# Layer norm 1 folded into transposed tiles, and the per-layer gate in blocks of 512 columns, in a one-core encoder layer

## What is computed

```python
h = layer_norm(ALPHA * x + merged @ w_out, ln1_g, ln1_b)      # merged: attention | SSM, each RMS-normed
pg_top, g_idx = top_k(softmax(h @ w_rg + b_rg), 1)            # 1 of 4 expert groups
pe_top, e_idx = top_k(softmax(selected h @ w_re + b_re), 2)   # 2 of its 8 experts
moe = sum over the two: gate * (silu(h @ w_gate[e]) * (h @ w_up[e])) @ w_down[e]
ple = sigmoid(h @ ple_w_gate) * (p @ ple_w_proj)              # the "per-layer" term, 2048 x 2048 and 256 x 2048
y   = layer_norm(ALPHA * h + moe + ple, ln2_g, ln2_b)
```

## Time and profile before

| | us |
|---|---|
| median of three runs | 1750.66 |
| profiled execution: its own time | 1749.11 |
| profiled execution: span | 1747.4 |
| TensorE busy | 1497.4 (86%) |
| VectorE busy | 532.8 (30%) |
| expert weights in the chain that ended last | 43% of the span |

### The profile page before, as it was taken

The page is one execution under the profiler, slowest core; times in us unless marked ns, Lnnn a source line. Parts: engine busy times, 40 slices in busy tenths (PEclk is TensorE's granted clock), DMA queues, the critical chain, the costliest instruction groups (busy, mean ns, idle before and its releaser), DMA issues.

```text
span 1747.4 us, 23011 instructions
## 1 busy us (share of the span) xinstructions
PE 1497.4 (86%) x8676; PEld 960.7 (55%) x8676; DVE 532.8 (30%) x1000; ACT 160.3 (9%) x321; POOL 242.8 (14%) x373
## 2 busy tenths in 40 slices
PE   5999999999998689879879779789778789787773
PEld 3677777777777565545545445445445445444341
DVE  6899998873101521001001001001000010110107
ACT  3011111114000200000000000000000000000001
POOL 3666666600000210000000000000000000000003
PEclk9999999999999589999989999999999899999996
DMA  6554545433594268999999999999999999999973
GB/s 176 136 146 109 148 112 142 114 106 105 184 302 149 68 227 316 417 411 397 419 408 395 418 408 403 411 408 413 393 408 417 396 406 415 410 409 414 403 281 135
DMA packets 202834, 521.34 MB, mean 298 GB/s; under 512 B 23184, under 2 KB 171760, under 8 KB 175280
## 3 DMA queue, kind: packets, MB, share of 16 engines
q1 hardware_dynamic: 187552, 487.79, 73.7%
q10 hardware_dynamic: 13120, 17.90, 3.3%
q0 software_dynamic: 2128, 15.21, 3.0%
HBM read 498.91 MB, written 21.95 MB: 298 GB/s over the span
## 4 chain that ended last, share of the span: by engine, by line
DMA 46%; PE 33%; DVE 10%; issue 4%; SPq 4%; POOL 1%; ACT 0%; DVEq 0%; ACTq 0%; POOLq 0%
DMA e_ring<-in_w_exp_up_dram 43%; PE bank L975 13%; PE bank L1264 8%; SPq L580 3%; PE bank L1195 2%; DMA e_ring<-in_w_exp_down_dram 2%; PE bank L1125 2%; DVE e_ring L1467 2%; SPq L552 1%; PE bank L1283 1%; PE bank L1017 1%; PE bank L1248 1%; PE bank L1009 1%; DVE e_ring L1471 1%; PE bank L986 1%
## 5 line engine op out<-in xcount | busy, mean ns | idle before, releaser
L1264 PE MATMUL bank<-e_ring,xT_exp 128*64 128x256 f32 x4096 | 496.9, 403 | 144.7 <-DMA e_ring<-in_w_exp_gate_dram 110.8
L1264 PEld LDWEIGHTS bank<-e_ring,xT_exp 128*64 128x64 f32 x4096 | 305.0, 145 | 347.4 <-DMA e_ring<-in_w_exp_gate_dram 133.7
L975 PE MATMUL bank<-xT,w_ring 128*128 128x288 f32 x1024 | 258.0, 411 | 0.7 <-issue 0.7
L1283 PE MATMUL bank<-e_ring,hidT 128*64 128x512 f32 x1024 | 228.0, 596 | 17.8 <-DVE hidT L1746 16.6
L975 PEld LDWEIGHTS bank<-xT,w_ring 128*128 128x128 f32 x1024 | 193.1, 191 | 56.9 <-issue 5.1
L975 PE MATMUL bank<-hT,w_ring 128*128 128x288 f32 x896 | 221.6, 408 | 0.0
L1741 DVE TENSOR_TENSOR hid<-bank,sig_exp 128x256 f32<-128x256 f32 x32 | 13.6, 424 | 627.7 <-ACT sig_exp L926 627.7
L975 PEld LDWEIGHTS bank<-hT,w_ring 128*128 128x128 f32 x896 | 170.1, 191 | 46.1
L720 POOL DMA_INDIRECT e_ring<-expert_rows_out,idx x6 | 5.5, 925 | 1075.5 <-ACT all_stored_mark L749 1074.0
L1283 PEld LDWEIGHTS bank<-e_ring,hidT 128*64 128x64 f32 x1024 | 69.6, 137 | 154.1 <-issue 118.4
L1752 DVE COPY rows<-bank 128x512 f32<-128x512 f32 x32 | 22.1, 692 | 221.7 <-PE bank L1283 221.7
(11 more groups left out here) (298 smaller groups left out, 1138.6 us busy)
## 6 DMA issues: line engine op xcount, KB each, us to landing
e_ring<-in_w_exp_gate_dram SPq DMA_DIRECT2D x64, 2048.0 KB, 24.1
e_ring<-in_w_exp_up_dram SPq DMA_DIRECT2D x64, 2048.0 KB, 25.6
e_ring<-in_w_exp_down_dram SPq DMA_DIRECT2D x64, 2048.0 KB, 26.0
w_ring<-in_w_in_dram SPq DMA_DIRECT2D x32, 1024.0 KB, 6.1
w_ring<-in_w_out_dram SPq DMA_DIRECT2D x16, 1024.0 KB, 7.0
w_ring<-in_w_ple_gate_dram SPq DMA_DIRECT2D x16, 1024.0 KB, 24.7
expert_rows_out<-hT POOLq DMA_DIRECT2D x3, 1536.0 KB, 9.5
w_ring<-in_ssm_w_glu_dram SPq DMA_DIRECT2D x4, 1024.0 KB, 5.0
```

The source lines that it names most:

```text
L975: last_mm = pe.matmul(out, weights(k), moving[:, k, :], start=(k == 0), stop=(k == n - 1))
L1264: mm = pe.matmul(gu[h * B:(h + 1) * B, s % 2, :], xT_exp[:, c, s // 2, :], w[:, c, h * FH:(h + 1) * FH], start=(s == 0 and c == 0), stop=( ...
L1283: mm = pe.matmul(bank[h * B:(h + 1) * B, 3 + n, :], hidT[:, c, half, :], e_ring[:, 2 * (NGU + half) + c, h * DH2 + n * 512:h * DH2 + (n + ...
```

## The change

It has five parts.

1. **Turning into rows** (`natural`) moves into the `w_out` loop: after block `m`, TensorE turns chunk `m - 1` of tile 0, and of tile 1 for chunks under 8. VectorE takes quarter statistics between the blocks.
2. **Gain and bias of layer norm 1** are no longer applied to the rows. They are applied per partition where `hT` is copied out of PSUM: ScalarE for even groups of four chunks (`hT_even`), VectorE for odd ones (`hT_odd`), with three banks in turn. The rows stored by expert are the normalised rows; so each expert's `x_copy`, now wholly on VectorE, multiplies by the gain and adds the bias over 128 x 1024 values.
3. **The per-layer gate** is cut into 4 blocks of 512 columns, and a block's contraction into 4 pieces of 512 rows. A piece is still 1 MiB, but 128 x 4 x 512: contiguous runs of 2 KiB rather than 512 bytes. The sums stay in PSUM banks 5 to 7 over the pieces, one piece a pair; the fourth group of 128 columns lies in two leftovers of 224 and 64 tokens, so a piece has 20 matmuls rather than 16. One projection (10 matmuls) closes a block. Block 0 is loaded before expert 1; pieces 0 to 2 are multiplied before the first expert, piece 0 ahead of the ranks. 12 pieces follow in the loop. The ln2 broadcasts are loaded after pieces 1 and 2, without the wait for the first expert's rows.
4. **The projection's load** sits in a block's second pair, where its slot has long been free.
5. **The final norm**: the sum over a row comes with the addition (`accum_out`), ScalarE sums the squares, and VectorE applies mean and gain, then root and bias, in two passes a tile. GpSimd takes only the root.

Loads and stores of an expert's rows also wait inside the branch on their size; the hidden rows are turned in bank 0.

The diff, cut to its core:

```diff
+        def ple_part(n):
+            if n < 3:
+                return ((bank[:, 5 + n, 0:T], 0, T, True),)
+            return ((bank[:, 5, T:512], 0, PLE_SPLIT, False), (bank[:, 6, T:2 * T - PLE_SPLIT], PLE_SPLIT, T, False))
...
+        def turn_bank(n):
+            return 4 + n % 3
...
-            sp.dma_start(w_ring[:, 2, :], ln1_g[0].partition_broadcast(P)).then_inc(gb1_landed, 16)
-            sp.dma_start(w_ring[:, 3, :], ln1_b[0].partition_broadcast(P)).then_inc(gb1_landed, 16)
...
+            def ple_gate_load(n, j, slot, wait):
+                sp.wait_ge(dense_done, wait)
+                settled()
+                sp.dma_start(w_ring[:, slot, :].rearrange("p (k n) -> p k n", k=4),
+                             w_plg_v[:, 4 * j:4 * j + 4, ds(n * (PLE_N * P), PLE_N * P)]).then_inc(w_landed[slot], 16)
...
+            ple_gate_load(0, 0, 0, N_PLE - 3)
+            ple_proj_load(0, N_PLE - 2)
+            ple_gate_load(0, 1, 2, N_PLE - 1)
+            ple_gate_load(0, 2, 3, N_PLE)
+            ple_gate_load(0, 3, 0, gate_done(0, 0))
+            sp.wait_ge(dense_done, gate_done(0, 1))
+            sp.dma_start(w_ring[:, 2, :], ln2_g[0].partition_broadcast(P)).then_inc(gb2_landed, 16)
+            sp.wait_ge(dense_done, gate_done(0, 2))
             sp.dma_start(w_ring[:, 3, :], ln2_b[0].partition_broadcast(P)).then_inc(gb2_landed, 16)
...
-            sp.wait_ge(xe_landed, 32)
-            sp.dma_start(w_ring[:, 2, :], ln2_g[0].partition_broadcast(P)).then_inc(gb2_landed, 16)
...
+            def load_pair(n, j):
+                ple_gate_load(n, j, 0, gate_done(n, j - 1) if j else gate_done(n - 1, PLE_N - 1))
+                if j == 1:
+                    ple_proj_load(n, proj_done(n - 1))
+                b = n * (2 * PLE_N) + (LEAD + 2 * j - 2 * PLE_N)
+                expert_load(b, b)
+                expert_load(b + 1, b + 1)
             expert_load(1, 1)
-            with sp.Fori(1, PLE_PAIRS) as i:
-                ple_load(i + EARLY_PLE, 0, 0, i * 2 + (N_PLE + 2 * EARLY_PLE - 1), i * 2 + (N_PLE + 2 * EARLY_PLE))
...
+            def hT_even(n):
+                t, q = n // 4, n % 4
+                act.wait_ge(hT_ready, n + 1)
+                for j in range(4):
+                    k = 4 * q + j
+                    a, b = vec_at["ln1_g"] + k, vec_at["ln1_b"] + k
+                    v = act.activation(hT[:, k, t * P:(t + 1) * P], bank[:, turn_bank(n), j * P:(j + 1) * P], ACT.Identity,
+                                       scale=vecT[:, a:a + 1], bias=vecT[:, b:b + 1])
+                v.then_inc(hT_act, 1)
...
+            for m in range(4, KC):
+                pe.wait_ge(w_landed[m % 4], m // 4 * 16 + 16 * (NCH + 2))
+                pe.wait_ge(res_ready, m - 1)
+                w = w_ring[:, m % 4, :].rearrange("p (k n) -> p k n", n=P)
+                dense(bank[:, 2 + m % 2, 0:T], lambda k: w[:, k, :], mergedT, KC).then_inc(dense_done, 1)
+                pe.wait_ge(res_ready, m)
+                for c in range(0 if m == 4 else m - 1, m):
+                    natural(0, c)
+                    if c < KC // 2:
+                        natural(1, c)
...
+            def turn(t, q):
+                t0, m = TT[t]
+                n = 4 * t + q
+                if n >= 3:
+                    pe.wait_ge(hT_dve if n % 2 == 0 else hT_act, (n - 3) // 2 + 1)
+                for k in range(KC if t == 2 else 4):
+                    mm = pe.transpose(bank[:, turn_bank(n), k * m:(k + 1) * m], rows[0:m, t, (4 * q + k) * P:(4 * q + k + 1) * P], ident[0:m, 0:m])
+                mm.then_inc(hT_ready, 1)
...
+            def ple_gate(n, j, slot, landed, early=False):
+                pe.wait_ge(w_landed[slot], landed)
+                if j == 0 and not early:
+                    pe.wait_ge(ple_mul, n)
+                w = w_ring[:, slot, :].rearrange("p (k n) -> p k n", k=4)
+                for c in (0, 1, 3, 2):
+                    if early and j == 0 and c == 2:
+                        pe.wait_ge(logits_read, 1)
+                    for out, t0, t1, opens in ple_part(c):
+                        for k in range(4):
+                            mm = pe.matmul(out, w[:, k, c * P:(c + 1) * P], hT[:, 4 * j + k, t0:t1],
+                                           start=(opens and j == 0 and k == 0), stop=(j == PLE_N - 1 and k == 3), skip_group_check=True)
+                mm.then_inc(dense_done, 1)
...
+            ple_gate(0, 0, 0, 16 * (NCH + 2 + KC // 4), True)
...
+            def pair(n, j):
+                b = n * (2 * PLE_N) + (LEAD + 2 * j - 2 * PLE_N)
+                expert(b, False, lambda: ple_gate(n, j, 0, n * (16 * PLE_N) + 16 * (NCH + 4 + KC // 4 + j - PLE_N)))
+                expert(b + 1, False, (lambda: ple_proj(n)) if j == PLE_N - 1 else None)
...
+            ple_gate(0, 1, 2, 16 * (NCH + 2 + KC // 4), True)
+            ple_gate(0, 2, 3, 16 * (NCH + 2 + KC // 4), True)
             pe.wait_ge(idx_ready, 1)
             x_turn(0)
-            pair(0, True)
-            with pe.Fori(1, PLE_PAIRS) as i:
...
+            for m in range(KC):
+                dve.wait_ge(dense_done, N_OUT + m + 1)
+                v = xT[:, m, :]
+                dve.scalar_tensor_tensor(out=v, in0=v, scalar=ALPHA, in1=bank[:, m if m < 4 else 2 + m % 2, 0:T], op0=ALU.mult,
+                                         op1=ALU.add).then_inc(res_ready, 1)
+                if m in (4, 8, 12):
+                    h_stats(0, m // 4 - 1)
+                if m in (4, 8):
+                    h_stats(1, m // 4 - 1)
+            h_stats(0, 3)
+            h_var(0)
+            h_stats(1, 2)
+            h_mean(0)
+            h_stats(1, 3)
+            h_var(1)
+            h_mean(1)
+            hT_odd(1)
+            hT_odd(3)
+            for q in range(4):
+                h_stats(2, q)
+            h_var(2)
+            hT_odd(5)
+            h_mean(2)
+            hT_odd(7)
+            dve.wait_ge(hT_ready, 9)
+            gb = [vecT[:, vec_at[v]:vec_at[v] + KC].unsqueeze(2).to_broadcast([P, KC, TS]) for v in ("ln1_g", "ln1_b")]
+            own(dve.tensor_tensor(hT[:, :, TP:T], bank[:, turn_bank(8), :].rearrange("p (k n) -> p k n", k=KC), gb[0], ALU.mult))
+            own.wait()
+            dve.tensor_tensor(hT[:, :, TP:T], hT[:, :, TP:T], gb[1], ALU.add).then_inc(hT_dve, 1)
...
             def x_copy(b):
                 dve.wait_ge(xeT_ready, b + 1)
-                dve.tensor_copy(xT_exp[:, 4:8].rearrange("p k h n -> p (k h n)"), bank[:, 2, :]).then_inc(xeT_dve, 1)
+                gx, bx = (gain_x[:, i].rearrange("p h c -> p c h").unsqueeze(3).to_broadcast([P, RUN, 2, B]) for i in range(2))
+                dve.tensor_tensor(xT_exp[:], bank[:, 1:3, :].rearrange("p b (c h n) -> p (b c) h n", h=2, n=B), gx, ALU.mult).then_inc(xeT_gain, 1)
...
+            def fin_add(t):
+                m = TT[t][1]
                 dve.wait_ge(y2_gathered[t], 16)
                 dve.wait_ge(fin_nat, t + 1)
                 b0 = 4 * (t % 2)
                 v = y_fin[0:m, t, :]
                 dve.scalar_tensor_tensor(out=v, in0=v, scalar=gate2[0:m, t:t + 1],
                                          in1=bank[0:m, b0:b0 + 4, :].rearrange("p b n -> p (b n)"),
-                                         op0=ALU.mult, op1=ALU.add).then_inc(fin_sum, 1)
+                                         op0=ALU.mult, op1=ALU.add, accum_out=row_sum[0:m, t:t + 1]).then_inc(fin_sum, 1)
...
+            def fin_scale(t):
+                m = TT[t][1]
+                dve.wait_ge(fin_nm, t + 1)
+                dve.wait_ge(fin_sq, t + 1)
+                v = y_fin[0:m, t, :]
+                dve.tensor_scalar(var_eps[0:m, t:t + 1], row_sq[0:m, t:t + 1], 1.0 / D, LN_EPS, ALU.mult, ALU.add).then_inc(fin_var, 1)
+                dve.scalar_tensor_tensor(out=v, in0=v, scalar=neg_mean[0:m, t:t + 1], in1=w_ring[0:m, 2, :],
+                                         op0=ALU.add, op1=ALU.mult).then_inc(fin_g, 1)
+                dve.wait_ge(fin_g, t + 1)
...
-                v = y_fin[0:m, t, SHARE:D]
-                dve.tensor_tensor(v, v, w_ring[0:m, 3, SHARE:D], ALU.add).then_inc(fin_b_dve, 1)
+                dve.scalar_tensor_tensor(out=v, in0=v, scalar=rstd[0:m, t:t + 1], in1=w_ring[0:m, 3, :],
...
+            fin_add(0)
+            fin_add(1)
+            fin_scale(0)
+            fin_add(2)
+            fin_scale(1)
+            fin_scale(2)
```

More of the change, by code:

```diff
@@ L382, in build @@
         res_ready = sem("res_ready")
-        nat_ready = sem("nat_ready")
+        nat_ready = [sem(f"nat_ready{t}") for t in range(NT)]
         var1_ready = sem("var1_ready")
@@ L598, in _ @@
+            expert_load(1, 1)
+            with sp.Fori(1, PLE_BLOCKS) as n:
+                for j in range(PLE_N):
+                    load_pair(n, j)
+            with sp.Fori(PLE_END, NE) as b:
                 expert_load(b, b)
@@ L953, in _ @@
             x_load(0)
-            x_copy(0)
-            x_load(1)
-            pair(0, True)
```

(21 more changed lines are left out.)

357 lines of the change are left out of this document (149 added, 208 removed).

## The result

The changed kernel takes **1733.11 us**, the median of four runs (1732.35 to 1734.78); the kernel before, four runs on the same chip, 1750.13. The ratio is 0.9904 (95% interval 0.9876 to 0.9932). So it is faster, as forecast, but by 17 us and not by 36: the forecast was 1714.7 and the range ended at 1731.

A forecast was written before the change was run, and what follows sets the result against it. The DMA weight stream was taken to bound the experts, with TensorE slack; gains of 3.4 + 4.6 + 4.3 + 13.1 + 10.6 = 36.0 us off 1749.1 gave 1713.1, median 1714.7 us, range 1702 to 1731.

The forecast's parts named there:

- Longer runs: Per-layer gate loads among the experts: runs of 2 KiB save 1.09 us a block, 13.1 us over 12 blocks.
- larger loop bodies: Expert loop: bigger bodies cost nothing, since queued weight pieces cover them.
- The prediction's own sign: Wrong if DMA share in the pairs falls under 1 or first expert to last piece shrinks by less than 9 us.
- The run length as a rival: Gate loads: run length doesn't matter, so the 13.1 us gain is missing and time is 1727.8; chance 0.15.
- The start: From w_out to the first expert: logits 11.4 us earlier, less later losses, so the first expert starts 3.4 us earlier.
- Ranks: After the logits: the gate's first piece goes ahead of the ranks on TensorE, costing 2.0 us (0 to 4.5).
- Sorting stores: Before expert 0's rows: the ln2 gain and bias loads fall into the stores, costing 4.0 us (0 to 5.6).
- The rival of the hole: Before the experts: slow clock, late ranks and both broadcasts cost 8.1 us more, time 1722.8; chance 0.10.
- The wait for the projection: Early experts: SP no longer stands waiting for the projection before a gate load, saving 4.6 us.
- One block fewer: Expert loop: 12 gate pieces follow instead of 13 blocks, saving 4.3 us.
- TensorE as the bound: Expert pairs: at a mean clock of 0.78 TensorE bounds them and the kernel is slower, 1790; chance 0.03.
- The end: Final norm: 24.0 us from first addition to last pass instead of 34.6, saving 10.6 us (9 to 12.5).

The follow-up runs named there:

- e1: The kernel before, with its 1 MiB gate loads read in runs of 2 KiB (wrong gate weights): 1740.19 us, ratio 0.9960.
- e3: The changed kernel with its gate loads read in runs of 512 bytes as before (wrong gate weights): 1737.18 us, ratio 0.9928.
- e7: The changed kernel with loop bodies of two pairs instead of four, sums opened by products with zeros: 1721.68 us, ratio 0.9842.
- e9: The changed kernel with loop bodies of two pairs and gate pieces in runs of 512 bytes (wrong gate weights): 1734.15 us, ratio 0.9917.
- e10: The changed kernel with the edits of e7 and e8 together: 1711.81 us, ratio 0.9801.
- e2: The kernel before, with its loop over pairs of experts written out in full on all engines: 1754.22 us, ratio 1.0026.
- e6: The kernel before, with both gate loads in runs of 2 KiB (wrong weights) and the pairs written out: 1752.40 us, ratio 1.0028.
- e5: The changed kernel with the loads of ln2 gain and bias held back until expert 0's rows have landed: 1726.65 us, ratio 0.9873.
- e4: The changed kernel with expert rows copied half on ScalarE, half on VectorE, without gain and bias: 1729.26 us, ratio 0.9882.
- e8: e5 plus ranks ahead of the first gate piece, block 0's last piece held back too, and hidT copied before x_copy: 1723.15 us, ratio 0.9856.

## Why the prediction was wrong, point by point

**Longer runs, −13.1: the main miss.** That run length has a price was right, and the earlier trace rows pointed to it: 0.79 us a block (e1) where I took 1.09, 0.79 × 12 = 9.5. But in the changed kernel as it stands it comes to next to nothing: 2.6 us over ten blocks (e3), which is within the noise. The step that failed is another one.

**"Nothing: larger loop bodies, with the queued pieces as cover."** I had asked whether an engine would stand still, and priced only that. No engine stood still: from 810 to 1480 every wait of TensorE in the changed kernel is for a landed piece, `hid` or `hidT`. The code itself comes through the DMA engines, in a stretch that they bound, and there it undoes the gain of the runs: 11.5 us between the changed kernel and e7 in the stretch 5 to 25, of a cause that I had put at zero. With the 3.2 us by which e7 falls short of the forecast there, the smaller price of the run, this makes up the 14.7. The term could have been bounded from below at nothing and from above at the whole −13.1. The prediction's own sign came true: it was to be wrong if the time from the first expert to the last piece shrank by less than 9 us, and from the first expert's matmul to the last sigmoid it shrank by 6.9 (1040.2 to 1033.3).

Here the Trainium skill has something that I had not drawn on. "Runtime: NRT & Kernel Launch", section Instruction fetch mechanics, says that TensorE's instruction memory holds 2048 instructions and is refilled in blocks of 16 KiB. The traces agree: the packets of the queue are 16 KiB, a pair of the changed kernel is 384 matmuls, as the trace counts them, and as many weight loads, 768 instructions; two pairs (1536) fit and e7 fetches little, four (3072) don't and the changed kernel fetches 36 packets. (Not all of it fits: e9, with the bodies of e7, fetches 21 packets and e10 4, and no run says why.) The same section calls the cost of crossing a block "mostly hidden" and says that kernels prefer full unrolling where possible. In this stretch the runs say otherwise: writing out costs 3.3 us (e2), and 11.1 us where the loads have long runs (e6 against e1).

**The run length as a rival (1727.8)** gave the nearest number for the wrong reason. It goes by the rule in the Trainium skill, "DMA: Bandwidth & Descriptors", section Specifications (512 B as the minimum for line rate); by e1 a MiB in runs of 512 bytes costs 0.8 us more than in runs of 2 KiB, so the trace disagrees, unless the price is on the places and not on the run.

**The start, −3.4: got −0.5.** The logits came 31.0 us after the last `w_out` product (563.87), where 30 was forecast. That this is so near is partly luck: tile 1 was turned back 13.5 us after the product and not 16.5, and then the router for tiles 0 and 1 took 12.1 us and not 7.5, at a granted clock of 0.57 (577.2 to 589.4). But that product ended 4.3 us later than before, not 3.0. Some 1.6 us of that look like this execution's own: the input projection starts at 37.36, while in e3, e5 and e7, with the same code up to there, it starts at 35.70 to 35.78. One issue of SP at 3.23 took 1.30 us where the others take 0.42; that this is the whole cause isn't shown. (This profiled execution is also the slowest of the four, 1.7 us over the median.) In e3, e5 and e7 the product ends 2.3 to 3.7 us later than before, about the 3.0 of the forecast. Ranks: +1.7 for a forecast of 2.0. Sorting stores: +5.1 (23.5 against 18.5 us) for 4.0, and e5 shows that the two broadcasts are the cause. `x_copy`: +1.9 for 2.0. So −9.1 + 1.7 + 5.1 + 1.9 = −0.4 (−0.5 by the rows; the rest is rounding). This comes to 2.9 us less than forecast: 1.3 by the later product, 1.0 by the way to the logits and 1.1 by the stores, less 0.4 by ranks and `x_copy` (the rows are rounded). The rival of the hole was right in one of its three parts, the broadcasts (5.1 of its 5.6). The slow clock that it gave as a reason did come, at the router, and the faster turns made up for it.

**The wait for the projection, −4.6**: two experts, sigmoid 1 to sigmoid 3, take 57.8 us instead of 63.5, −5.7. Right in place and roughly in size. **One block fewer, −4.3**: experts 25 to 27 take 62.9 instead of 66.0, −3.1.

**TensorE as the bound: wrong, as expected.** It is busy 57.4 us a pair at a mean clock of 0.95, within 67.4.

**The end, −10.6: got −9.0, and 2.0 lost ahead of it.** From the first addition to the last pass's end is 24.0 us, exactly as summed:

```profile
1699.27 10.12 PE L1387 MATMUL bank<-e_ring,pT 128*128 128x512 f32 x16 [4.10 <-DMA e_ring<-expert_rows_out,idx]
...
1706.11 2.35 DVE L1872 SCALAR_TENSOR_TENSOR e_ring<-e_ring,gate,bank 128x2048 f32<-128x2048 f32 x1 [17.16 <-PE bank L1387]
...
1727.75 2.34 DVE L1889 SCALAR_TENSOR_TENSOR e_ring<-e_ring,rstd,w_ring 32x2048 f32<-32x2048 f32 x1 [0.51 <-POOL rstd L745]
```

1706.11 to 1727.75 + 2.34 is 24.0. What came short lies before it. The additions wait for the first eight matmuls, which took 6.8 us here and 5.37 before. TensorE had idled for 4.10 us here and 3.77 before, and the mean granted clock over these eight was 0.56 here (1699.3 to 1706.1) and 0.68 before (1704.3 to 1709.6). The 2.0 us ahead are the wait behind `x_copy` at the last expert, with the slow clock that followed it (e4). I had costed that wait, "1.8 us an expert of the 10.7 a pair", with the stream as its cover, and not asked what it costs where the stream ends.

**Range.** Its lower side took the bounds; its upper side left out a full loss of the run term together with a poor start (1734 in the text). The loss of the run term happened in full, by a cause that was not among the cases; of the poor start about half did, and the end gave up the rest.

## What to carry to other kernels

Where a stretch is bound by DMA, the program's own code is traffic in it, and here it cost more than its bytes: count the instructions of a loop body on each engine, look for the instruction queues in the window in question, and keep TensorE's body small, if need be by a loop over pieces whose sums a product with zeros opens. A transfer that nobody waits for, such as the ln2 weights here, still costs when it is issued beside one that somebody waits for; one wait on the rows gave some 6 us. For each wait that is costed at nothing because of a cover, name the first and the last iteration, where the cover is missing.

## What the runs showed of the hardware that was not expected

Run length and code fetches don't add. Without fetches, runs of 2 KiB instead of 512 bytes give 7.9 us over ten blocks of 1 MiB; with them, 0.1 (e2, e6) to 2.6 (e3), neither of them clear of nothing. Fetches cost 3.3 us beside short runs and 11.1 beside long ones, for 31 packets of 16 KiB and 14 of 8 KiB, whose 0.62 MB would take 1.5 us at 407 GB/s. The loss is not a pure matter of their number either: e7 has 12 of the large packets in the window, and is as fast as e1 with none. Why this is so stays open. A load is waited for until all its parts have landed, so that a single delayed DMA engine could hold it up while the mean share stays at 1.01. This is a guess. For it: in the last 6 us before the last sigmoid of the changed kernel the share is 0.55 (1668 to 1674), while TensorE still waits for an up piece, and so it is in e4, e5 and e8 with the same bodies and runs (0.53 to 0.57), but not in e7 (1.01). Against it: e6 has the full loss and no such tail (0.96 from 1677 to 1683). The trace gives no share by DMA engine, and no run here tells this apart.
